# Output projection and feed-forward joined into one stage: plain float32 matmuls on 128-token tiles in place of split three-pass matmuls on 104-token tiles

## What is computed

```python
def _merge(fox_o, gla_o, gr, gla_norm_g, w_out):
    gn = gla_o * lax.rsqrt(jnp.mean(jnp.square(gla_o), axis=-1, keepdims=True) + EPS)
    gated = gn.reshape(B, T, GLA_VW) * gla_norm_g * jax.nn.silu(gr)
    mix = jnp.concatenate([fox_o, gated], axis=-1)
    return mix @ w_out                                  # 1024 x 1024

def _swiglu(h, w_gate, w_up, w_down):                   # 1024 x 2816, 1024 x 2816, 2816 x 1024
    return (jax.nn.silu(h @ w_gate) * (h @ w_up)) @ w_down

y = y + _merge(...)
y = y + _swiglu(_rmsnorm(y, norm2_g), w_gate, w_up, w_down)
out = _rmsnorm(y, final_norm_g)
```

## Time and profile before

| | us |
|---|---|
| median of 3 runs | 3926.75 |
| lowest, highest | 3926.39, 3927.2 |
| span of the profiled execution | 3927.2 |
| that execution's own time | 3927.2 |

### The profile page before, as it was taken

One profiled execution on the slowest core, in us unless ns is written; L12 is line 12 of the kernel. 1 busy time (PEld: TensorE's weight loads), 2 busy tenths in 40 slices (PEclk: granted clock), 3 DMA queues, 4 the chain that ended last, 5 costly groups with the idle time before them and its releaser, 6 DMA issues. The chain is left out here.

```text
span 3927.2 us, 50875 instructions
## 1 busy us (share of the span) xinstructions
PE 3380.7 (86%) x18752; PEld 2990.7 (76%) x18752; DVE 2257.7 (57%) x3597; ACT 999.1 (25%) x1699; POOL 597.8 (15%) x379
## 2 busy tenths in 40 slices
PE   6999999398998995455559969999999699999996
PEld 5999999255555553355547759999999599999996
DVE  5001111455555553388834347877877577877876
ACT  5111111234444441244422221111111211112112
POOL 0000000000000000277600032122221312122220
PEclk9999999689999997677779979999999799999997
DMA  3223222211110107112134441111111421111113
GB/s 103 80 76 91 55 65 55 55 19 24 25 27 16 27 1 227 29 60 60 47 119 135 126 124 43 48 47 44 48 43 46 129 68 43 48 47 44 48 32 93
DMA packets 244878, 247.23 MB, mean 63 GB/s; under 512 B 37209, under 2 KB 206569, under 8 KB 239617
## 3 DMA queue, kind: packets, MB, share of 16 engines
q1 hardware_dynamic: 243465, 241.96, 20.9%
q10 hardware_dynamic: 1344, 4.36, 0.5%
HBM read 179.49 MB, written 66.79 MB: 63 GB/s over the span
## 5 line engine op out<-in xcount | busy, mean ns | idle before, releaser
L2026 PE MATMUL ps_ffn<-h,wsp_n 128*128 128x312 f32 (+1 forms) x6336 | 1056.8, 323 | 43.8 <-POOL h L1862 28.9
L2026 PEld LDWEIGHTS ps_ffn<-h,wsp_n 128*128 128x128 f32 x6336 | 1017.5, 189 | 50.2 <-issue 38.1
L1961 DVE TENSOR_TENSOR yacc<-ps_ffn,yacc 128x312 f32<-128x312 f32 (+1 forms) x1056 | 494.9, 514 | 223.0 <-PE ps_ffn L2041 223.0
L361 PE MATMUL ps_project<-hT,wsp 128*128 128x416 f32 x3000 | 579.7, 354 | 3.2 <-DVE wsp L327 3.2
L361 PEld LDWEIGHTS ps_project<-hT,wsp 128*128 128x128 f32 x3000 | 561.7, 189 | 12.0 <-issue 4.9
L2041 PE MATMUL ps_ffn<-aT,dsp 128*128 128x312 f32 (+1 forms) x3168 | 545.1, 321 | 9.7 <-DVE yacc L1961 9.7
L2041 PEld LDWEIGHTS ps_ffn<-aT,dsp 128*128 128x128 f32 x3168 | 508.5, 188 | 12.4 <-issue 9.7
L752 PE MATMUL ps_fox<-pt,va 128*65 128x512 f32 (+3 forms) x640 | 307.5, 568 | 55.9 <-DVE osb L871 47.5
L1857 POOL TENSOR_TENSOR wsp_n<-wraw_n,wsp_n 128x1024 fp32r<-128x1024 f32 x88 | 210.7, 2395 | 802.8 <-ACT wsp_n L1898 802.8
L1928 ACT ACTIVATE aT<-a 128x416 fp32r<-128x416 f32 x132 | 65.2, 494 | 1003.9 <-DVE a L1983 1003.9
L737 PE MATMUL ps_fox<-qk_split 65*128 65x512 f32 (+3 forms) x960 | 275.8, 428 | 48.6 <-DVE qk_split L876 42.2
(11 more groups left out here) (210 smaller groups left out, 3200.3 us busy)
## 6 DMA issues: line engine op xcount, KB each, us to landing
wraw_n<-in_w_gate_dram SPq DMA_DIRECT2D x44, 512.0 KB, 3.8
wraw_n<-in_w_up_dram SPq DMA_DIRECT2D x44, 512.0 KB, 3.8
draw<-in_w_down_dram SPq DMA_DIRECT2D x44, 512.0 KB, 3.5
zT<-zs SPq DMA_DIRECT2D x12, 1040.0 KB, 4.7
wraw<-in_w_in_dram SPq DMA_DIRECT2D x24, 512.0 KB
x<-x2s SPq DMA_DIRECT2D x20, 416.0 KB
h2T<-hT_m SPq DMA_DIRECT2D x20, 416.0 KB
hraw<-h2T SPq DMA_DIRECT2D x20, 416.0 KB
```

What stands on the lines that cost most here:

```text
L361: last = pe.matmul(ps[:, g, 0:BLK], wsp[:, b, s, k, :], hT[:, g * TPB:(g + 1) * TPB, v, k, :], start=m == 0, stop=m == 3 * KD - 1)
L1961: dve.tensor_tensor(y, ps[:, 4 + i, 0:FB[b] * TT], y, ALU.add).then_inc(added, 1)
L2026: last = pe.matmul(ps[:, 2 * q + s, 0:FB[b] * TT], wsp[:, par, s, w, k, :], h2[:, FB0[b]:FB0[b + 1], v, k, :], start=m == 0, stop=m == 3 * ...
```

## The change

`merge` and `ffn` are replaced by one stage, `tail`.

- Tokens go in 17 tiles, 16 of 128 and one of 32 (`NTILE`, `tile_rows`). There are no HI and LO tensors: every matmul takes plain float32 operands, one instruction per product.
- The projection of tile t is 16 matmuls of 512 columns (L1835), with 8 transposes ahead and 8 behind. Roots are taken on GpSimd with a power of -0.5 (L1654 to L1663).
- The feed-forward takes the tokens in four chunks of 512, 512, 512 and 544 columns (`CHUNK_COLS`). In each chunk all 22 blocks of gate and up come first (L1862), 16 matmuls of 512 columns a block, in the last chunk 32 of 272. ScalarE applies Silu in one instruction (L1714), VectorE multiplies (L1786) into a full `aT` of all 22 blocks.
- Then come the down products of the chunk, tile by tile: 2 x 22 matmuls of 512 columns that accumulate in PSUM (L1881), with `w_down` resident in SBUF. It is loaded during the first chunk, into the space (`arena`) that the projection used. VectorE adds x2 (L1794), then the last norm, and the rows are stored. There is no `yacc` and no transposing back.
- `w_gate` and `w_up` are read four times in place of twice, through three buffers (`GUB`).

```diff
-def merge(nc, d):
-            def middle(t, b):                                   # TensorE
-                for n in range(2):
-                    m = 0
-                    for k in range(KD):
-                        for s, v in PASSES:
-                            last = pe.matmul(ps[0:TT, 2 + 2 * b + n, :], mT[:, b, s, k, :], wsp[:, v, k, n * 512:(n + 1) * 512],
-                                             start=m == 0, stop=m == 3 * KD - 1)
-                            m += 1
...
-def ffn(nc, d):
...
+NTILE = NTOK // P + 1
+NF = DFF // P
+CHUNK_TILES = ((0, 4), (4, 8), (8, 12), (12, NTILE))
+CHUNK_COLS = ((0, 512), (512, 512), (1024, 512), (1536, 544))
+SUBS = (((0, 512),), ((0, 512),), ((0, 512),), ((0, 272), (272, 272)))
+XR = 4
+GUB = 3
...
+def tail(nc, d):
+        arena = sb("arena", [P, NF * D])
+        wgu = sb("wgu", [P, GUB, 2, KD, P])
+        h2T = sb("h2T_n", [P, KD, CMAX])
+        aT = sb("aT", [P, NF, CMAX])
+        xy = sb("xy", [P, XR, D])
...
+            def load_gu(g):                                     # SP
+                f, s = g % NF, g % GUB
+                if g >= GUB:
+                    c0, f0 = divmod(g - GUB, NF)
+                    sp.wait_ge(up_done, units_before(c0, f0) + len(SUBS[c0]))
+                sp.dma_start(wgu[:, s, 0], wg[:, :, f * P:(f + 1) * P]).then_inc(gu_come[s], 16)
+                sp.dma_start(wgu[:, s, 1], wu[:, :, f * P:(f + 1) * P]).then_inc(gu_come[s], 16)
...
+            load_mix(0)
+            load_x(0)
+            sp.dma_start(grow2, d["norm2_g"].partition_broadcast(P)).then_inc(g_in, 16)
+            for k in range(KD):
+                sp.dma_start(wout[:, k], d["w_out"][0, k * P:(k + 1) * P, :]).then_inc(w_come, 16)
+            load_mix(1)
+            load_x(1)
+            sp.dma_start(growf[:], d["final_norm_g"].partition_broadcast(P)).then_inc(f_in, 16)
+            for g in range(GUB):
+                load_gu(g)
...
+            for c, (t0, t1) in enumerate(CHUNK_TILES):
+                for f in range(NF):
+                    if NF * c + f + GUB < NF * len(CHUNK_TILES):
+                        load_gu(NF * c + f + GUB)
+                    if c == 0:
+                        sp.dma_start(wd[:, f], d["w_down"][0, f * P:(f + 1) * P, :]).then_inc(d_come, 16)
+                    if f == NF - 4:
+                        for t in range(t0, t0 + XR):
+                            load_r(t)
+                if c + 1 < len(CHUNK_TILES):
+                    load_h2(c + 1)
+                for t in range(t0, t1):
+                    store_y(t)
...
+                    act.activation(silu[:, u % 2, 0:n], ps[:, 4 * (u % 2), 0:n], ACT.Silu).then_inc(silu_done, 1)
...
+            def project_out(t):                                 # TensorE
+                for a in range(2):
+                    for k in range(KD):
+                        last = pe.matmul(ps[0:n, 2 + 2 * b + a, :], mT[:, b, k, 0:n], wout[:, k, a * 512:(a + 1) * 512],
+                                         start=k == 0, stop=k == KD - 1)
...
+            def gate_up(c, f, s):
+                else:
+                    pe.wait_ge(a_made, u - 1)
+                for w, done in ((0, gate_done), (1, up_done)):
+                    for k in range(KD):
+                        last = pe.matmul(ps[:, 4 * (u % 2) + w, 0:n], wgu[:, g % GUB, w, k, :], h2T[:, k, c0:c0 + n],
+                                         start=k == 0, stop=k == KD - 1)
+                    last.then_inc(done, 1)
...
+            def down(c, t):
+                if t == 0:
+                    pe.wait_ge(d_come, 16 * NF)
+                for a in range(2):
+                    for f in range(NF):
+                        if a == 0 and t == CHUNK_TILES[c][0]:
+                            pe.wait_ge(a_made, units_before(c, f) + len(SUBS[c]))
+                        last = pe.matmul(ps[0:n, bank + a, :], aT[:, f, col:col + n], wd[:, f, a * 512:(a + 1) * 512],
+                                         start=f == 0, stop=f == NF - 1)
+                    last.then_inc(down_done, 1)
...
-    merge(nc, d)
-    ffn(nc, d)
+    tail(nc, d)
```

More of the change, by code:

```diff
@@ L1477, in _, with tile_rows, units_before @@
             close(NCH - 1, 1, CH)
-def merge(nc, d):
+NTILE = NTOK // P + 1
[3 more added lines that the diff above has]
+SUBS = (((0, 512),), ((0, 512),), ((0, 512),), ((0, 272), (272, 272)))
+CMAX = 544
+XR = 4
+GUB = 3
+def tile_rows(t):
+    return P if t < SEQ // P else NEW
+def units_before(c, f):
+    return NF * c + f if c < 3 else NF * 3 + 2 * f
+def tail(nc, d):
     with ExitStack() as ctx:
         sb, sem, psum = scope(nc, ctx)
-        ident = sb("ident_m", [P, P])
[L1488 to L1511, removed]
-        block = ctx.enter_context(nc.Block())
[L1513 to L1541, removed]
@@ new lines, in _ @@
+            load_mix(1)
[3 more added lines that the diff above has]
+                load_gu(g)
+            for i in range(NTILE + 2):
+                if i + 2 < NTILE:
+                    load_mix(i + 2)
+                    load_x(i + 2)
+                if 0 <= i - 1 < NTILE:
+                    store_x2(i - 1)
+                if 0 <= i - 2:
+                    store_h(i - 2)
+                if i == 9:
+                    load_h2(0)
@@ L2068, in _, with turn, turn_mix @@
-            steps(pe, lambda: None, step, True, final)
+            def turn(rows, n, bank0):
+                for k in range(KD):
+                    last = pe.transpose(ps[:, bank0 + k // 4, (k % 4) * P:(k % 4) * P + n], rows[0:n, k * P:(k + 1) * P], ident[0:n, 0:n])
+                return last
+            def turn_mix(t):
+                pe.wait_ge(m_ready, t + 1)
+                if t >= 1:
+                    pe.wait_ge(mt_a, t)
+                    pe.wait_ge(mt_b, t)
+                turn(mix[:, t % 2], tile_rows(t), 0).then_inc(m_turned, 1)
@@ new lines, in _ @@
+            for i in range(-1, NTILE):
+                if i + 1 < NTILE:
+                    turn_mix(i + 1)
+                if i >= 0:
+                    project_out(i)
+                if i - 1 >= 0:
+                    turn_h(i - 1)
+            gate_up(0, 0, 0)
+            turn_h(NTILE - 1)
+            for c, (t0, t1) in enumerate(CHUNK_TILES):
+                for f, s in units(c):
+                    if c or f:
+                        gate_up(c, f, s)
+                for t in range(t0, t1):
+                    down(c, t)
```

672 lines of the change are left out of this document (256 added, 416 removed).

## The result

The changed kernel takes 4162.11 us (median of 4 runs, 4161.57 to 4163.05), the kernel before took 3926.57 beside it (4 runs, 3925.8 to 3927.2): a ratio of 1.06, with an interval of 1.0585 to 1.0615. It is 6.0% slower; 4174 us, 6.3% slower, was forecast, and the time lies in the range of 4155 to 4212. The profiled execution took 4162.15 us for a span of 4160.4.

A forecast was written before the change was run, and what follows sets the result against it. TensorE was taken as the bound. Of 1941.8 us at stake, matmuls add 379.4 and the rest saves 131.8, giving 2189.4; with 1985.4 kept that is 4174.8, predicted as 4174 us, range 4155 to 4212.

The forecast's parts named there:

- What stays: Everything before the changed stage keeps its instructions: 1985.4 us stay, 1941.8 us are at stake.
- the launch term: Stage start to first projection: 22.6 us, bounds 15 to 30, putting that projection near 2008.
- Matmuls: Plain float32 in projection, gate and up, and down: 2109.2 us against 1729.8, so 379.4 us more.
- Launch, transposes and the third mix tile: Start of the new stage: launch 22.6 us, transposes 29.6, slow first projection 2, third mix tile wait 6.
- The wait of 6 us for the third mix tile: Tile queued behind 3 MB of gate and up blocks on SP: 6 us, between 0 and 12.
- `w_down`: TensorE waits once, before the first down product, for the last block: 10 us, between 7 and 14.
- End: Last addition, square, norm and store at the program's end: 10 us, between 8 and 14.
- Costed at nothing: Silu in one instruction, dropped yacc additions, streamed weights and h2T transfers in the feed-forward: no time gained or lost.
- the 212 us: Non-matmul part of the old 1941.8 us: launches, transposes, first splits, half turn, end; forecast to become 80.2 us.
- plain float32 at another pace: Rival at all 2780 new matmuls: cheaper in long streams, so the kernel comes out faster; 3%.
- Transfers did not fall behind: Rival in chunk 0: 1.5 MB needs over 13.76 us, each of 22 units waits; 4256 us at 90 GB/s; 4%.
- The clock was held: Rival: TensorE at 1.2 GHz for part of the stage, 100 us more per 100 us of work; 3%.

The follow-up runs named there:

- the fast kernel: Changed kernel with split three-pass float32r feed-forward, five chunks, streamed weights, first two w_down blocks split one unit earlier; 3782.54 us, 0.9632 of the kernel before.

## Why the prediction was right

Forecast by the profiled execution 4174.8 us, measured 4162.15: a span of 4160.4 us and 1.75 us outside it, which the sum did not have. Inside the span 14.4 us were forecast too much. By the prediction's steps:

- **What stays.** 1985.4 us were carried over and the stage started at 1983.9. I counted the launch from 1985.4, so the launch term took up the difference. In the ten traces this point lies anywhere between 1981.8 and 1987.7, behind the same instructions, so no single term here is tested to less than some 2 us.
- **Matmuls, 2109.2 us (+379.4).** Gate and up: 302.5 us in chunk 0 without its transposes, 302.13 twice, 322.66: 1229.4, not 1232.0. Down: 153.39 + 151.07 + 151.07 + 440 x 0.4291 = 644.3, not 643.3, with 2.3 us of it from the halved clock behind the wait. Projection with its slow first tile: 235.8 up to the first gate and up matmul without transposes, where 233.9 + 2 was forecast. In all 1.7 us less. A pace read off four records of 512 columns held over 4152, and the one worked out for 272 columns, 0.230, over 1408 (0.2292). The arithmetic alone in the old structure cost 378 us, so this term was not right by a cancellation.
- **Launch, transposes and the third mix tile.** First projection at 2008.58, forecast 2008. The 0.6 us are luck: from the start of the stage it was 24.7 us and not 22.6, and the stage started 1.5 us early. From there to 2271.42 are 262.8 us, forecast 269. The wait of 6 us for the third mix tile never came, and this is the step that failed. In order of time:

```profile
2004.66 0.19 POOL L1654 TENSOR_SCALAR gq<-gq 128x4 f32<-128x4 f32 x1 [15.77 <-DMA gq<-gsq]
...
2012.23 1.89 SPq L1547 DMA_DIRECT2D arena<-mixf  x1
...
2019.22 0.19 POOL L1654 TENSOR_SCALAR gq<-gq 128x4 f32<-128x4 f32 x1 [13.26 <-DMA gq<-gsq]
```

  The third tile came 14.6 us behind the second, where I had some 21, and TensorE turned to it only at 2024.38. SP was held up behind 3 MB of gate and up blocks, as I had thought, and single issues took up to 6.46 us; but from 2000 to 2030 the transfers ran at 277 GB/s and not at the 181 that I had priced. About 2 us more are transposes of the first two mix tiles, which I had counted both in the launch and in the 29.6.
- **`w_down`.** 7.13 us, forecast 10 from 7 to 14: at its lower bound, since from 2574.5 to 2581.6 the transfers ran at 269 GB/s and not at the 181 that I had priced. With 2.3 us of lower clock, already in the down term, it cost 9.4.
- **End.** 440 records from 3964.11 end near 4152.9, so 7.5 us, forecast 10 from 8 to 14: just below its lower bound. Up to the last scaling it went as priced, 3.1 us for the 3.2 allowed; 32 rows save nothing there, for the addition took 0.68 us and the square 1.05 as with 128 rows. From the last scaling on it was 4.4 us, not 6.8: the span ended 3.1 us after the last store was issued, before it was 5.1. Why the store landed sooner stays open.
- **Costed at nothing.** Borne out: TensorE had 280.00 of 280 us with Silu and without. The old structure, where I did not look, had 16 us of it at its turns; in the sum they are part of the 212 us and needed no term.

These make 1.7 + 7.4 + 2.9 + 2.5 = 14.5 us of the 14.4 (7.4 is the 6 and the 2, less the 0.6 by which the first projection was late). The 212 us of everything else became 67.5, not 80. All four groups erred to the same side, so the total is not good by cancellation among them.

The rivals: plain float32 at another pace is excluded by 0.4291 us a record over 4152. The pace of 131 ns that the Trainium skill gives for 512 columns ("TensorE: Matmul & The Clock Gate", "Back-to-back issue gap") matches neither this nor the float32r records of 0.2325. Transfers did not fall behind: TensorE did not wait inside any chunk, and gate and up took 302.5 us in chunk 0 and 302.13 in the next two, although the transfer share is highest in chunk 0 (0.40, then 0.30). The clock was held: 1.00 in each chunk, 0.99 over the stage.

What the change does is therefore two things of opposite sign. Against the kernel before, the plain float32 pass costs 378 us, and the structure gives 143. With the split kept, the structure gives 144 us (3927 to 3783), although `w_down` is loaded five times and the split still has to be done. That the two are so close is chance: the second still has the plain float32 projection, some 11 us dearer (233.9 against 223.2), and streams its weights otherwise. What was not tried is the projection with three passes in the fast kernel: 17 x 48 x 0.2325 = 190 in place of 234 us, an estimate from the earlier trace rows, and it needs room in SBUF for the split `w_out`.

## What to carry to other kernels

Price a change of data type on the engine that is the bound, by the start-to-start pace of records of that very type, before counting what it frees elsewhere: here one plain float32 matmul (0.858 us) replaced three float32r passes (0.70 us), and halving VectorE's and GpSimd's work bought nothing inside the chunks, only at the launch and the turns. Take a change with two mixed effects apart (the new arithmetic in the old structure, the old arithmetic in the new one), since the part worth keeping may hide under the part that loses: the new structure with the old arithmetic gave 3783 us, below both 3927 and 4162. And price a stall of the matmul engine with what the clock takes after it, and look for stalls at the turns between phases, where the last item of a queue decides.

## What the runs showed of the hardware

- One plain float32 matmul of 512 columns leaves two records of 0.4291 us, 0.858 us in all: 4 cycles a column at 2.4 GHz (853 ns) and 5 ns; at 272 columns it is 458 ns, 453 and 5. A float32r pass of 512 columns takes 232.5 ns in the projection before, one cycle a column (213 ns) and 19 ns. In the long streams of the last kernel it is less: 1008 records from 2281.44 to 2510.05 are 226.8 ns each, and 1056 of 384 columns from 2630.91 to 2813.97 are 173.4, both one cycle a column and 13.4 ns. Three passes against one are 3 to 4 in cycles, but 0.81 in time (0.79 in the long streams), since each float32r pass has that surcharge.
- A gap of TensorE of 3.05 us cost 4.5 to 4.8, one of 3.58 cost 6.3 and one of 7.13 cost 9.4 (the gap and the longer matmuls behind it). But one of 3.14 us cost only 3.7, one of 3.31 in the kernel before nothing beyond itself (at 3054.09: 4.78 us for 24 matmuls, elsewhere 4.71), and one of 2.73 with Silu in the kernel before 1.6 us more (at 3047.29: 6.35 us for 24). The length of a gap alone does not say what it costs. Behind the 3.58 us PEclk was 0.50 for 3.6 us and 0.74 in the 4 us after.
- While the 3 MB of gate and up blocks were going out at the launch, single issues on SP took 3.96 and 6.46 us; at the end of chunk 0 they took 0.37 to 1.26. It delayed nothing here.
- ScalarE's Silu took 597 ns at 512 columns and 398 ns at 272, so its price is on the line of the 519 ns that exp took at 416. GpSimd's power of 32x1 took 0.53 us, the one of 128x4 at the launch 1.03.
